# Two chained transformer blocks on one core: the double norm before the hybrid mixer with its residual scaled later, its steps in a new order, and the mixer's norm weight multiplied into weight blocks on GpSimd

## The reference, cut to what matters

```python
def rmsnorm(x, w):            # first block; second block: rms_norm, the same with fp32 gain
    return x * rsqrt(mean(x * x, -1) + 1e-6) * w

def conv_ffn(h, w_up, conv_w, conv_b, w_down):
    u = causal_dwconv(h @ w_up, conv_w, conv_b)
    g, val = split(u, 2)
    return (silu(g) * val) @ w_down

def first_block(x, ...):
    x = x + gla_mixer(rmsnorm(x, mix_norm_w), ...)
    x = x + conv_ffn(rmsnorm(x, ffn_norm_w), ...)
    return rmsnorm(x, final_norm_w)

def hybrid_mixer(h, ...):
    xa, ga, q, f, v, g, m_a, m_b = split(h @ w_in, 8)      # w_in is 1024 x 8192
    ...                                                     # an RG-LRU branch and an HGRN2 branch
    return y @ w_out

# second block, on the output x of the first
x = x + hybrid_mixer(rms_norm(x, norm_mix), ...)
x = x + square(relu(rms_norm(x, norm_mlp) @ w_up)) @ w_down
out = rms_norm(x, norm_final)
```

## Time and profile before

| | us |
|---|---|
| median of 3 runs | 2998.28 |
| lowest and highest | 2997.21, 3000.92 |
| the profiled execution | 2997.87 |
| its span (first to last instruction) | 2995.1 |
| mean granted TensorE clock | 0.966 of full speed |
| PE busy | 2807.6 (94% of the span) |
| POOL busy | 1624.7 (54%) |
| DVE busy | 1550.7 (52%) |
| ACT busy | 1044.1 (35%) |

### The profile page before, as it was taken

The page is one execution under the profiler, slowest core; times in us unless marked ns, Lnnn a source line. Parts: engine busy times, 40 slices in busy tenths (PEclk is TensorE's granted clock), DMA queues, the critical chain, the costliest instruction groups (busy, mean ns, idle before and its releaser), DMA issues. The chain is left out here.

```text
span 2995.1 us, 38841 instructions
## 1 busy us (share of the span) xinstructions
PE 2807.6 (94%) x13675; PEld 2323.1 (78%) x13675; DVE 1550.7 (52%) x1972; ACT 1044.1 (35%) x1484; POOL 1624.7 (54%) x1096
## 2 busy tenths in 40 slices
PE   5999997799999999589999999999998999999998
PEld 4888786688888887467777777777777788888886
DVE  4233425355555555846566566566444344444445
ACT  3213215333333333434444444443524222222222
POOL 3332333577677765665465465565433656555552
PEclk8999998899999999799999999999999999999999
DMA  3110110121111112111121121111250111111112
GB/s 115 36 50 28 42 42 0 35 57 54 51 49 56 56 49 70 60 46 35 54 61 33 56 60 32 57 57 36 77 190 8 50 49 56 56 56 45 46 49 84
DMA packets 200853, 160.62 MB, mean 54 GB/s; under 512 B 6246, under 2 KB 176827, under 8 KB 200763
## 3 DMA queue, kind: packets, MB, share of 16 engines
q1 hardware_dynamic: 200763, 159.35, 17.6%
HBM read 143.60 MB, written 15.73 MB: 53 GB/s over the span
## 5 line engine op out<-in xcount | busy, mean ns | idle before, releaser
L312 POOL TENSOR_TENSOR w_lo<-w_raw,w_hi 128x512 fp32r<-128x512 f32 x280 | 393.6, 1412 | 310.1 <-ACT w_hi L306 309.9
L408 PE MATMUL PA<-h_hi,w_hi 128*128 128x512 f32 x840 | 352.6, 420 | 61.1 <-ACT hy_gm L2338 19.9
L409 PE MATMUL PA<-h_lo,w_hi 128*128 128x512 f32 x840 | 340.1, 405 | 0.0
L410 PE MATMUL PA<-h_hi,w_lo 128*128 128x512 f32 x840 | 339.3, 404 | 0.0
L312 POOL TENSOR_TENSOR w_lo<-f_sums,w_hi 128x512 fp32r<-128x512 f32 x114 | 168.5, 1478 | 168.8 <-ACT w_hi L306 168.8
L306 ACT CAST w_hi<-w_raw 128x512 fp32r<-128x512 f32 x280 | 168.7, 616 | 245.4 <-DMA w_raw<-in_w_in 115.8
L408 PEld LDWEIGHTS PA<-h_hi,w_hi 128*128 128x128 f32 x840 | 166.0, 198 | 104.4 <-issue 35.1
L408 PE MATMUL PB<-f_t_hi,w_hi 128*128 128x512 f32 x560 | 220.9, 395 | 1.7 <-ACT hy_tm L2341 0.9
L410 PE MATMUL PB<-f_t_hi,w_lo 128*128 128x512 f32 x560 | 218.3, 390 | 0.0
L409 PE MATMUL PB<-f_t_lo,w_hi 128*128 128x512 f32 x560 | 217.9, 389 | 0.0
L312 POOL TENSOR_TENSOR w_lo<-w_lo_raw,w_hi 128x512 fp32r<-128x512 f32 x108 | 140.4, 1307 | 128.9 <-ACT w_hi L306 128.9
(11 more groups left out here) (469 smaller groups left out, 7139.1 us busy)
## 6 DMA issues: line engine op xcount, KB each, us to landing
w_raw<-in_w_in SPq DMA_DIRECT2D x64, 512.0 KB, 5.3
w_raw<-in_ffn_w_up SPq DMA_DIRECT2D x44, 512.0 KB, 4.6
w_raw<-in_w_up SPq DMA_DIRECT2D x32, 512.0 KB, 5.3
w_lo_raw<-in_w_down SPq DMA_DIRECT2D x64, 256.0 KB, 2.5
w_raw<-in_gla_w_in SPq DMA_DIRECT2D x24, 512.0 KB, 3.7
w_lo_raw<-in_ffn_w_down SPq DMA_DIRECT2D x44, 256.0 KB, 2.6
X<-in_x SPq DMA_DIRECT2D x8, 512.0 KB, 6.6
w_raw<-in_gla_w_out SPq DMA_DIRECT2D x8, 512.0 KB, 3.5
```

What stands on the lines that cost most here:

```text
L312: pool.tensor_tensor(lo, source, hi.bitcast(F32), ALU.subtract).then_inc(self.split, 1)
L408: pe.matmul(bank, ah[:, k, :], bh[:, k, :], start=(k == 0 and not more), stop=False, skip_group_check=more)
L409: pe.matmul(bank, ah[:, k, :], bl[:, k, :], start=False, stop=False, skip_group_check=more)
L410: mm = pe.matmul(bank, al[:, k, :], bh[:, k, :], start=False, stop=(k == 3), skip_group_check=more)
```

## The change

Four things:

1. **The hybrid's norm weight.** norm_mix becomes eight columns `C_NH` of the parameter table (one more short load at the start), and the hybrid's ring weighs its raw tiles with it on POOL. The first pair is weighed in the tail (`begin`), the other 31 in the hybrid's loop: 62 instructions of 128x1024. ACT's high parts of P1, P2 and P4 and the first sum now wait for it. In exchange `scale` multiplies by the scalar rs alone (a tensor_scalar).
2. **The residual.** L688 is gone. X · final_norm_w is stored as soon as POOL has made it; r1 is kept in a table of its own (`r1`), and the out-projection's additions become x · r1 + product, once for each half of the columns.
3. **The tail's order.** The arrivals of the last row tiles are spread between the transposes, DVE and ACT take their steps in another order, and a dummy square root loads ACT's table early.
4. **The end of f1.** The last product of gate and value (`prod`) moves from the sixth to the fourth of eight steps on DVE, and ACT's casts of the last down weights go ahead of its last cast of activations.

```diff
-    def __init__(self, sem, name, core, xn, T, ready, rows, small):
+    def __init__(self, sem, name, core, xn, T, ready, row, small):
...
-        for q in range(-2, 4):
-            if -1 <= q < 3:
-                squares_again(q + 1)
+        act.activation(c.sd[:, 0:1], c.zero, ACT.Sqrt)
+        square(0)
+        square(1)
+        square_again(0)
+        square(2)
+        square_again(1)
+        root(0)
+        square(3)
+        for q in range(4):
+            high(q, *self.MADE[:3])
+            if q < 3:
+                square_again(2 * q + 2)
+                square_again(2 * q + 3)
                 root(q + 1)
...
+            if q < 2:
+                square(2 * q + 4)
+            high(q, *self.MADE[3:5])
+            if q < 2:
+                square(2 * q + 5)
+            high(q, *self.MADE[5:])
...
         def scale(q, two):
-            inverses = self.inverses[:, q, :]
+            second = self.inverses[:, q, 2:4]
             dve.wait_ge(self.roots, q + 1)
-            dve.reciprocal(inverses, self.sds[:, q, :])
+            dve.reciprocal(c.r1[:, two], self.sds[:, q, 0:2])
+            dve.reciprocal(second, self.sds[:, q, 2:4])
...
-                dve.scalar_tensor_tensor(out=self.x(k).rearrange("p (b s) -> p b s", s=P),
-                                         in0=c.X[:, self.ORDER[k], :].rearrange("p (b s) -> p b s", s=P),
-                                         scalar=c.rs[:, k:k + 1], in1=self.rows[1], op0=ALU.mult, op1=ALU.mult).then_inc(done, 1)
+            scaled(2 * q, self.scaled_even)
...
+        def scaled(k, done):
+            self.free(dve, k)
+            dve.tensor_scalar(self.x(k), c.X[:, self.ORDER[k], :], c.rs[:, k:k + 1], None, ALU.mult)\
+               .then_inc(done, 1)
...
-                for h in range(2):
-                    x = c.X[:, self.ORDER[2 * q + 2 + h], :]
-                    dve.tensor_scalar(x, x, self.inverses[:, q + 1, h:h + 1], None, ALU.mult).then_inc(self.residual, 1)
+                scale_odd(q + 1)
...
-            sp.wait_ge(self.residual, k + 1)
+            sp.wait_ge(self.weighed, k + 1)
...
-                tail.gpsimd(pool, lambda: ahead.pair_low(pool, 0, 0, 0, "first"))
+                
+                def begin():
+                    ahead.weigh(pool, 0)
+                    ahead.pair_low(pool, 0, 0, 0, "first")
+                tail.gpsimd(pool, begin)
...
                 down_high(chunks, 0, 0, 1)
                 last_high(0)
+                down_high(chunks, 1, 0, 1)
                 last_high(1)
-                down_high(chunks, 1, 0, 1)
...
-                        if m == 5:
+                        if m == 3:
                             prod(i, u)
...
-        return Ring(sem, "hy", self.core, sums, None, 56, 56, 56 * (HG_HEADS // 2))
+        return Ring(sem, "hy", self.core, sums, C_NH, 56, 56, 56 * (HG_HEADS // 2))
...
                             begun = isinstance(i, int) and i == 0 and k == 0
+                            if not begun:
+                                ring.weigh(pool, i * 8 + k)
...
+                def scaled_add(x, m, product_):
+                    k = tail.ORDER.index(m)
+                    return dve.scalar_tensor_tensor(out=x, in0=x, scalar=c.r1[:, k:k + 1], in1=product_,
+                                                    op0=ALU.mult, op1=ALU.add)
...
-                        dve.tensor_tensor(x, x, part[b], ALU.add).then_inc(s["part_add"], 1)
+                        scaled_add(x, m, part[b]).then_inc(s["part_add"], 1)
...
-                        dve.tensor_tensor(x, x, down_bank(c, n, 4), ALU.add).then_inc(s["down_add"], 1)
+                        if h:
+                            scaled_add(x, m, down_bank(c, n, 4)).then_inc(s["down_add"], 1)
+                        else:
+                            dve.tensor_tensor(x, x, down_bank(c, n, 4), ALU.add).then_inc(s["down_add"], 1)
```

More of the change, by code:

```diff
@@ L56 @@
 C_NM = C_NF + 8
-C_END = C_NM + 8
+C_NH = C_NM + 8
+C_END = C_NH + 8
 ROWS = 4 * FT
@@ L591, in scalar, with square, square_again @@
         junk = c.tlo[:, 0:MT, 3 * P:4 * P]
-        def square(k, out, done):
+        def square(k):
+            act.wait_ge(*self.ready(k))
+            wait(act, self.squared, k)
+            wait(act, self.squared_again, (0, 0, 1, 2, 4, 4, 6, 6)[k])
             act.activation(junk, c.X[:, self.ORDER[k], :].rearrange("p (b s) -> p b s", s=P),
[L595 to L609, removed]
+                           ACT.Square, accum_out=c.ss[:, k:k + 1]).then_inc(self.squared, 1)
+        def square_again(k):
+            act.wait_ge(self.weighed, k + 1)
+            act.wait_ge(self.squared, (2, 3, 4, 4, 6, 6, 8, 8)[k])
+            wait(act, self.squared_again, k)
+            act.activation(junk, c.X[:, self.ORDER[k], :].rearrange("p (b s) -> p b s", s=P),
+                           ACT.Square, accum_out=c.ms[:, k:k + 1]).then_inc(self.squared_again, 1)
         def high(q, *names):
@@ L702, in weigh @@
         pool.wait_ge(self.squared, k + 1)
-        pool.tensor_tensor(x, x, self.rows[0], ALU.mult).then_inc(self.weighed, 1)
+        pool.tensor_tensor(x, x, self.row, ALU.mult).then_inc(self.weighed, 1)
     def gpsimd(self, pool, late):
-        pool.wait_ge(self.row_in[0], 16)
-        for q in range(-1, 4):
-            if q < 3:
-                for h in range(2):
-                    self.weigh(pool, 2 * q + 2 + h)
+        pool.wait_ge(self.row_in, 16)
+        for q in range(-2, 4):
             if q == 3:
@@ L1440, in tile, with last_tile @@
                     for k in range(2):
-                        if isinstance(i, int) and i == chunks:
-                            left = last_hi[k][:, m, :], last_lo[k][:, m, :]
-                        else:
-                            left = ahi[k][:, m * P:(m + 1) * P], alo[k][:, m * P:(m + 1) * P]
+                        left = ahi[k][:, m * P:(m + 1) * P], alo[k][:, m * P:(m + 1) * P]
                         mm = product(pe, banks(n), left, ring.slot(i, p + k), k == 0, k == 1)
+                    return mm
+                def last_tile(m, h, n):
+                    pe.wait_ge(s["down_add"], (chunks - 1) * DOWN + max(n - 2, 1))
+                    for k in range(2):
+                        mm = product(pe, banks(n), (last_hi[k][:, m, :], last_lo[k][:, m, :]),
+                                     ring.slot(chunks, down_at(chunks, h) + k), k == 0, k == 1)
                     return mm
@@ L1463, in last @@
                     for h in range(2):
-                        tile(chunks, tail.ORDER[k], h, 2 * k + h).then_inc(s["down_mm"], 1)
+                        last_tile(tail.ORDER[k], h, 2 * k + h).then_inc(s["down_mm"], 1)
                 tail.tensor(pe, last)
```

64 lines of the change are left out of this document (35 added, 29 removed).

## The result

| | before | after |
|---|---|---|
| median, us | 2998.28 (5 runs) | 3016.93 (5 runs) |
| lowest to highest | 2994.0 to 3000.92 | 3015.43 to 3023.98 |
| the profiled execution | 2997.87 | 3020.16 |

After to before is 1.0068, with a 95% interval of 1.0054 to 1.0082: 18.6 us slower, above the range of 2986 to 3014. In the lines after the change, L363 is the weigh of blocks (L362 before), L615 the square root (L619), L678 the scaled tile (L668), L717 the weigh of X (L703), L409 to L411 the pair products (L408 to L410).

A forecast was written before the change was run, and what follows sets the result against it. PE's work plus its gaps set the time, tail edits being paid almost in full and hybrid edits only where they delay PE. 2997.9 − 14 (tail) + 18 (hybrid) + 0.3 (parameter load) = 3002.2, so 3002 us; range 2986 to 3014.

The forecast's parts named there:

- What bounds the kernel: Whole kernel: PE's work plus its gaps; tail edits paid almost in full, hybrid edits only where they delay PE's next product.
- The end of f1, −2: End of f1: earlier casts of the last down weights shorten PE's wait for POOL's low parts; −2 us, bounds 0 and 3.
- The tail's turns, −11: Tail: DVE gives up work, POOL is late next, turns take 12 to 13 us; −11 us (−9 to −14).
- The end of the tail, −0.5: Last root to the hybrid: shorter scaled tiles −3, POOL's two added weighs of blocks +2.5; about −0.5 us.
- The hybrid, late sums: Hybrid's fq, v and gm gates: weighs delay block sums, hence ACT's casts and drains; +14.4 us (8.7 to 20.7).
- the clock's 4: Hybrid's v gates: after longer waits PE restarts at the lower clock level; +4 us (0 to 8).
- The hybrid, VectorE: Hybrid: DVE held up by POOL's weighs; no term in the forecast's sum, left to rival B.
- rival B: Hybrid: weighs also hold VectorE, delaying combinations before drains at gb, v and gm gates; +9 or 10, 3012 us; chance 0.19.
- The sum: Whole kernel: 2997.9 − 14 + 18 + 0.3 = 3002.2, so 3002 us; chance 0.44, own range 2991 to 3009.
- A: Hybrid: it hides the weighs, with a loss of only 0 to 5 us; 2987 us; chance 0.26.
- C: Tail: it stays long, with turns of 15 us and a gain of only 5; 3011 us; chance 0.08.
- The rest: Out-projection's sixteen scaled additions 0 (3 if contended), and one more parameter load on SP +0.3 us.

The follow-up runs named there:

- first: The changed kernel with none of the hybrid's blocks weighed and norm_mix left out: 2985.19 us, 0.9954.
- fourth experiment: The changed kernel with the norm weight's row back in the tail's scaled tiles on DVE and no weighs in the hybrid: 2986.18 us, 0.9959.

## Why the prediction was wrong, step by step

- **What bounds the kernel.** Right: the tail is paid nearly in full, and the hybrid only at gates. But that POOL, busy 123 to 129 of 228, has room for the weighs asked only whether POOL has the time, not who reads beside it.
- **The end of f1, −2.** Right: −2.2 alone, and in the changed kernel PE's last down tiles start 1.9 us earlier, counted from f1's end.
- **The tail's turns, −11.** Mis-sized, and for a wrong reason. The four roots span 40.5 us (1207.91 to 1248.42) against 48.4, so −7.9. The scaled tiles cost 0.75, less than the 1.75 I took, and POOL was not the late engine: it still waited 21.2 us for ACT's square sums, 12.2 of them behind the first. Where I took a turn from an engine's busy sum (11.3), it was a chain. In the third turn: arrivals on DVE at 1222.24, square on ACT at 1223.55, weigh on POOL at 1224.78, second squares from 1227.19, mean squares on DVE from 1229.64, root at 1232.53, and DVE's next such arrivals at 1236.58.
- **The end of the tail, −0.5.** 14.0 us from the last root to the hybrid against 16.4, so −2.4; POOL's weighs at 1246.46 to 1250.2 stood beside the mean squares and stretched them. The whole tail −11.7 against −14: a miss of 2.3, within its range.
- **What the tail's gain is from.** Wrong in its attribution: the short scaled tiles gave 0 to 1 us, the residual 5.9 alone and the end of f1 2.2. The new order is left with 2.5 to 3.6, by subtraction only.
- **The hybrid, late sums.** Right in place and nearly in size. 14.4 + 4 was foreseen for the fq, v and gm gates, and 20.7 were lost to gm's first product: fq 6.3 (foreseen 3.3), v 9.7 (7.8), gm 4.8 (3.3), with the clock's 4 on top. At the first gate 2.0 was foreseen; PE's wait there went from 5.50 to 6.44, not 7.5, but its start against the hybrid's is 2.1 later. Some of the match is luck: at the v gates PE waited 0 to 0.9 us for L2327 and not 2 to 5, since in three passes it had already waited 1.7 to 2.3 us for DVE (L2429) at fq's sixth product, and the 20.7 hold a share of contention, which the sum had left out.
- **The hybrid, VectorE.** This is the step that failed. The forecast priced contention at 0 and left it to rival B, at 9 or 10 us, since I looked for it at the drains and in L2434 alone. The runs showed 7.1 us at the gb gate, where kernels with as much delay and less reading gain 2.9 to 4.8. It comes by the level chain: PE waited 16.6 us for L2368's drain against 19.9, and 12.4 instead of 2.4 for the levels. The chain's rows in the trace before, PE's wait of 0.54 us, 0.69 and 1.22 us in the two instructions ahead, looked cheap because POOL mostly stood still beside them, waiting for tiles (4.73 us until 1369.86). It is that wait which the weighs fill. The passes came to 234.7, 237.9, 235.7 and 234.0 us, against 229, 233, 231 and 233.
- **The sum.** From the traces 2997.9 − 11.7 + 20.7 + 7.1 + 2.5 (rest of the passes) + 0.8 (behind the hybrid, not explained) = 3017.3. Without the gb gate and the rest it is 3007.7, in the range. None of the rivals was priced as high as the result.
- **Rival B.** The mechanism was right, its price a little low, its place and its signs off. By its sum 3012. The convolution's line L2469 has a median of 2060 and not above 2.1, though two of its instructions went from 1.28 to 2.66 us beside weighs, and PE's longest wait at a gb gate is 4.62, just above 4.6, in one pass of four; in the others it fell to 1.16, 3.02 and 3.18, because PE had waited earlier, for the level.
- **Rivals A and C.** A fell with the 20.7 us at the gates. C fell: turns of 13.5 us.
- **The rest.** 0.29 for the parameter load (7.38 to 7.67 at PE's first transpose) against 0.3. The scaled additions: 0, by the first and fourth experiment.

## What to carry to other kernels

Before work goes to an engine that has idle time, look at which of the other engine's instructions read two operands beside it, and whether a chain with PE hangs on those; an idle share says nothing of that, and a low price in the trace before may only mean that nobody read beside it. The median of a line that has two lengths does not tell what it costs; the wait of the engine behind it does. Multiplying a norm's weight into 32 pairs of weight blocks costs 31 us to save one in the tail; eight multiplications by a row, placed where the other engine waits, cost less. In a stage of a few turns through several engines, the length of the chain sets the turn, and it is worth adding that up before an engine's busy sum.

## What the runs showed of the hardware

- A two-input multiplication of 128x512 on DVE took 0.69 us alone and some 1.75 beside POOL's tensor_tensor on SBUF. Nine of them beside a memset on POOL alone took 0.68 or 0.69. A tensor_scalar of 128x1024 with one input went from 0.69 to 2.23 beside a weigh.
- A memset of 128x512 on POOL took 0.53 us, against 1.27 for a sum of the same shape and 1.90 for a weigh of 128x1024.
- The weigh lost nothing to contention in its median (1903 ns), but 22 of the 62 in the hybrid took over 2 us, 2954 ns at most: both sides wait.
- Block sums 2.3 us late cost 7 us over 31 pairs, 3.3 us late cost 25 (by memsets, with DVE's busy time 12 us up as well, which I can't separate).
